# Gated linear attention on 64-row matmuls: halves of the array instead of zero-padded operands

## The reference, cut to what matters

```python
def gla_chunked(q, k, v, log_a):          # C = 64
    b = jnp.cumsum(gc, axis=-2)
    ref = b[..., C // 2 - 1:C // 2, :]
    q_in = qc * jnp.exp(b - ref)
    k_in = kc * jnp.exp(ref - b)
    A = jnp.where(mask, jnp.einsum('nbhid,nbhjd->nbhij', q_in, k_in), 0.0)
    o_intra = jnp.einsum('nbhij,nbhjv->nbhiv', A, vc)
    q_inter = qc * jnp.exp(b)
    k_state = kc * jnp.exp(b_last - b)
    decay = jnp.exp(b_last[..., 0, :])
    def step(state, inp):
        o = jnp.einsum('bhid,bhdv->bhiv', qi, state)
        state = state * di[..., None] + jnp.einsum('bhjd,bhjv->bhdv', ki, vi)

o_f = gla_chunked(q, k, v, la_f)
o_b = flip(gla_chunked(flip(q), flip(k), flip(v), flip(la_b)))
o = rmsnorm(o_f + o_b, out_norm)
```

## Time and profile before

| | |
|---|---|
| median of three runs | 2820.85 us (2816.14 to 2821.78) |
| profiled execution | span 2816.3 us from first to last instruction; 30040 instructions |
| PE busy | 2493.3 us, 89% of the span |
| PE weight loads | 1792.1 us, 64% |
| DVE busy | 1210.0 us, 43% |
| ACT busy | 984.3 us, 35% |
| POOL busy | 471.9 us, 17% |
| granted PE clock, mean | 0.948 |

### The profile page before, as it was taken

The page is one execution under the profiler, slowest core; times in us unless marked ns, Lnnn a source line. Parts: engine busy times, 40 slices in busy tenths (PEclk is TensorE's granted clock), DMA queues, the critical chain, the costliest instruction groups (busy, mean ns, idle before and its releaser), DMA issues. The chain is left out here.

```text
span 2816.3 us, 30040 instructions
## 1 busy us (share of the span) xinstructions
PE 2493.3 (89%) x10658; PEld 1792.1 (64%) x10658; DVE 1210.0 (43%) x1936; ACT 984.3 (35%) x1573; POOL 471.9 (17%) x506
## 2 busy tenths in 40 slices
PE   5997787938999958898999989998889899998997
PEld 4876465823444436787766667776777766666875
DVE  3379575241111144454235543523555215554433
ACT  3211575110111144554422232425555333223413
POOL 4157142021222123111100000002111110000000
PEclk9999899978999969999999999998999999999998
DMA  3201100146999851010110021101110120003101
GB/s 93 79 30 60 60 1 9 39 112 223 352 338 321 286 210 39 23 28 25 40 56 10 1 90 60 36 38 48 30 30 23 31 71 20 0 1 120 65 4 60
DMA packets 207016, 222.64 MB, mean 79 GB/s; under 512 B 50464, under 2 KB 170528, under 8 KB 206880
## 3 DMA queue, kind: packets, MB, share of 16 engines
q1 hardware_dynamic: 196400, 204.02, 22.3%
q0 software_dynamic: 9440, 16.83, 1.7%
q10 hardware_dynamic: 1040, 0.00, 0.0%
HBM read 203.41 MB, written 33.13 MB: 84 GB/s over the span
## 5 line engine op out<-in xcount | busy, mean ns | idle before, releaser
L106 PE MATMUL ps<-WT_lo,HT_hi 128*128 128x512 f32 x832 | 326.5, 392 | 0.0
L107 PE MATMUL ps<-HT_hi,WF_lo 128*128 128x512 f32 (+1 forms) x800 | 316.1, 395 | 0.0
L105 PE MATMUL ps<-HT_hi,WU_hi 128*128 128x512 f32 (+1 forms) x704 | 288.6, 410 | 15.8 <-DVE H_lo L2016 12.4
L106 PE MATMUL ps<-H_lo,WU_hi 128*128 128x512 f32 (+1 forms) x704 | 277.0, 394 | 0.0
L1463 PE MATMUL ps<-WT,MIX 128*128 128x512 f32 x496 | 226.1, 599 | 2.9 <-DVE MIX L1974 2.9
L105 PE MATMUL ps<-W_hi,HT_hi 128*128 128x512 f32 x512 | 212.3, 415 | 6.4 <-DVE MIX_lo L2153 6.4
L874 POOL TENSOR_TENSOR WF_lo<-WF,WU_hi 128x1024 fp32r<-128x1024 f32 (+1 forms) x44 | 116.2, 2640 | 607.8 <-ACT WU_hi L1079 607.8
L107 PE MATMUL ps<-W_hi,MIX_lo 128*128 128x512 f32 x512 | 200.9, 392 | 0.0
L427 POOL TENSOR_SCALAR ss<-ss 128x1 f32<-128x1 f32 x56 | 15.5, 277 | 1041.3 <-ACT ps L415 786.7
L106 PEld LDWEIGHTS ps<-WT_lo,HT_hi 128*128 128x128 f32 x832 | 158.2, 190 | 36.4 <-issue 5.3
L107 PEld LDWEIGHTS ps<-HT_hi,WF_lo 128*128 128x128 f32 (+1 forms) x800 | 151.9, 190 | 34.1
(11 more groups left out here) (395 smaller groups left out, 4854.4 us busy)
## 6 DMA issues: line engine op xcount, KB each, us to landing
WT<-in_w_gate SPq DMA_DIRECT2D x31, 1024.0 KB, 5.9
WT<-in_w_up SPq DMA_DIRECT2D x31, 1024.0 KB, 9.4
MIX<-in_w_down SPq DMA_DIRECT2D x31, 1024.0 KB, 8.7
WF<-in_w_in SPq DMA_DIRECT2D x48, 512.0 KB, 3.9
WT<-in_w_out SPq DMA_DIRECT2D x6, 2048.0 KB, 9.0
H<-in_x SPq DMA_DIRECT2D x16, 512.0 KB, 6.9
h_dram<-H SPq DMA_DIRECT2D x16, 512.0 KB, 3.4
H<-h_dram SPq DMA_DIRECT2D x16, 512.0 KB, 6.9
```

The costliest lines, as they stand in the source:

```text
L105: pe.matmul(o, lh, rh, start=(i == 0), stop=False)
L106: pe.matmul(o, lh, rl, start=False, stop=False)
L107: mm = pe.matmul(o, ll, rh, start=False, stop=(i == last))
```

## The change

`kf` and `kb` become one tile `k_in` written by one DVE instruction over all 128 partitions, `ks_even` and `ks_odd` one tile `ks` written by two ACT instructions in place of four. `inner` and `states` take 64 partitions of both operands per matmul: first partitions 0 to 63, then 64 to 127, in turns, into different PSUM banks. The number of matmuls in them stays 16 each. `causal` adds `Af` and `Ab` into `Asum` on DVE, and `outputs` does three matmuls for a tile in place of four. POOL's two memsets get half as wide.

```diff
-        kf, kb = slot(WTf, 0), slot(WTf, 1)
+        k_in = slot(WTf, 0)
-        ks_even, ks_odd, Af, Ab = (MIX[:, i, :] for i in range(4))
+        ks, Asum, Af, Ab = (MIX[:, i, :] for i in range(4))
+        kv_pairs = kv.rearrange("p (t r) v -> p t r v", r=2)
@@ POOL
-                pool.memset(WT[:, 0, :, :], 0.0).then_inc(z_ready, 1)
+                pool.memset(WT[:, 0, 4:KD, :], 0.0).then_inc(z_ready, 1)
-                pool.memset(MIX[:, 0:4, :], 0.0).then_inc(z_ready, 1)
+                pool.memset(MIX[:, 2:4, :], 0.0).then_inc(z_ready, 1)
@@ ACT
                 def ks_copy(h):
                     act.wait_ge(*gla(L, "kt", h))
-                    act.wait_ge(z_ready, L * 5 + 2)
+                    if h == 0:
+                        act.wait_ge(mx_lo, mx_at(L, 0, NT - 1))
                     for half in range(2):
-                        act.activation(ks_even[0:64, half * HALF:(half + 1) * HALF], ps[0:64, 6 + half, :], ACT.Copy)
-                        o = act.activation(ks_odd[64:P, half * HALF:(half + 1) * HALF], ps[64:P, 6 + half, :], ACT.Copy)
+                        o = act.activation(ks[:, half * HALF:(half + 1) * HALF], bank(6 + half), ACT.Copy)
                 def kv_copy(h):
                     for b in range(4):
-                        o = act.activation(kv[:, 4 * b:4 * b + 4, :], quads(2 + b), ACT.Copy)
+                        half, par = b % 2, b // 2
+                        o = act.activation(kv_pairs[:, 4 * half:4 * half + 4, par, :], quads(2 + b), ACT.Copy)
@@ PE
-                    for d, kk in enumerate((kf, kb)):
-                        for t in range(NT):
-                            mm = pe.matmul(bank(2 + 2 * d + t // 4, P, (t % 4) * P), kk[:, t * P:(t + 1) * P], q_in[:, t * P:(t + 1) * P], start=True, stop=True)
+                    for t in range(NT):
+                        ts = slice(t * P, (t + 1) * P)
+                        for d in range(2):
+                            r = slice(64 * d, 64 * d + 64)
+                            mm = pe.matmul(bank(2 + 2 * d + t // 4, P, (t % 4) * P), k_in[r, ts], q_in[r, ts], start=True, stop=True)
                     for c in range(NCH):
-                        t = c // 2
-                        mm = pe.matmul(bank(2 + c // 4, P, (c % 4) * P), (ks_even, ks_odd)[c % 2][:, t * P:(t + 1) * P], gv[h % 2][:, t * P:(t + 1) * P], start=True, stop=True)
+                        t, par = c // 2, c % 2
+                        r, ts = slice(64 * par, 64 * par + 64), slice(t * P, (t + 1) * P)
+                        mm = pe.matmul(bank(2 + 2 * par + t // 4, P, (t % 4) * P), ks[r, ts], gv[h % 2][r, ts], start=True, stop=True)
-                        mm = accumulate(pe, ..., [(gv[h % 2][:, ts], Af[:, ts]), (gv[h % 2][:, ts], Ab[:, ts]),
+                        mm = accumulate(pe, ..., [(gv[h % 2][:, ts], Asum[:, ts]),
@@ DVE
-                    dve.tensor_tensor(kf[0:64, :], gt[0:64, :], k[0:64, :], ALU.mult)
-                    dve.tensor_tensor(kb[64:P, :], gt[64:P, :], k[64:P, :], ALU.mult)
+                    dve.tensor_tensor(k_in, gt, k, ALU.mult)
@@ causal, behind the masked copies
+                    dve.wait_ge(*gla(L, "am", h))
+                    if h >= 1:
+                        dve.wait_ge(*gla(L, "o", h - 1))
+                    dve.tensor_tensor(Asum, Af, Ab, ALU.add)
```

More of the change, by code:

```diff
@@ L1567, in outputs @@
                         ts = slice(t * P, (t + 1) * P)
-                        mm = accumulate(pe, bank(6 + t // 4, P, (t % 4) * P), [(gv[h % 2][:, ts], Af[:, ts]), (gv[h % 2][:, ts], Ab[:, ts]),
+                        mm = accumulate(pe, bank(6 + t // 4, P, (t % 4) * P), [(gv[h % 2][:, ts], Asum[:, ts]),
                                                                              (st[:, 2 * t, :], q_even[:, ts]), (st[:, 2 * t + 1, :], q_odd[:, ts])])
```

## The result

The changed kernel takes 2775.85 us, median of four runs (2774.13 to 2778.56), against 2820.63 (2816.14 to 2821.78) for four runs of the kernel before. The medians are 44.8 us apart; 41.6 were forecast. The ratio of the runs is 0.9847 (95% interval 0.9835 to 0.9859), which is 43.2 us less (39.8 to 46.5). In the profiled executions the span went from 2816.3 to 2772.4 us.

A forecast was written before the change was run, and what follows sets the result against it. PE was taken to bound the stretch behind the heads, and within heads PE alternating with ACT/DVE chains. Terms: -18.5 without overlap, -25.7 and +2.6 with it, together -41.6 us from 2820.85, giving 2779 us; range 2769 to 2808.

The forecast's parts named there:

- Side by side: inner and states: matmuls on the two array halves run together, a tenth lost; -25.7 us over 16 stages.
- rivals 1 and 2: inner and states: single file, no gain there, 2805 us (chance 0.25); or half overlapped, 2791 us (chance 0.15).
- rival 3: inner and states: every change of row group empties the pipe; slower, 2844 us; chance 0.07.
- the low clock: inner(0): with PE's wait ahead shortened, the low clock may not come; 3.8 us saved in all.
- The pipe at a change of size: Changing between 128-row and 64-row matmuls may empty the pipe, at most 0.163 us each; +2.6 us taken.
- outputs: outputs: 16 of 64 records go; -3.6 us behind head 3, -1.4 us from head 2's slack.
- products: One DVE instruction less: -4.9 us ahead of inner(1) and inner(3), -6.5 ahead of inner(0), -3.8 from its clock.
- The memset: Second layer's start: POOL's L874 comes earlier, meets DVE's row split and delays the first unit; +1.7 us taken.
- the waits were to stay ahead of `inner(1)` and `inner(3)`: Sign: PE's waits ahead of these stages still ended by ACT L1181, a little longer than before.

The follow-up runs named there:

- g1: Kernel before with only inner and states put on 64 rows in turns; products, copies, memsets and outputs kept: 2792.02 us.
- e1: Changed kernel with four products a tile in outputs again, Af and Ab one by one, no Asum: 2782.78 us.
- e2: Changed kernel with k_in written by two DVE instructions of 64 partitions each: 2794.62 us.
- e4: Changed kernel with POOL's memset of WT back at its old width, 8 slots in place of 4: 2775.29 us.
- e3: Changed kernel with the same matmuls not in turns, all of rows 0 to 63 first, then 64 to 127: 2804.47 us.
- h1: Changed kernel with the first block's attention scores also on 64 rows, the two halves in turns: 2770.25 us.

## Why the prediction was right, term by term

**Side by side** (forecast -25.7, with +2.6 for an emptied pipe). Right in mechanism; rivals 1 and 2 fall with the record cuts, rival 3 with the stages of 2.06 us. A stage falls from 3.73 to 2.06, 1.67 and not the 1.79 of the full halving: the second pair starts 0.21 us behind the first, and only the later ones at steps of 0.112. The size was off the other way: g1, which has this step alone, gains 28.1 where the two terms made 23.1. Part of it is the low clock. `inner` lost 13.2 us to it before (43.0 in eight stages, where 8 x 3.73 would be 29.8) and loses 9.3 in g1 (25.8 for 16.5).

**The pipe at a change of size** (forecast +2.6). The price is there, and a little above the prediction's bound of 0.163 us a change. `states(3)` stands between two units and shows it at the full clock, before and after:

```profile
1329.39 0.39 PE L107 MATMUL ps<-HT_hi,WF_lo 128*128 128x512 f32 x1
1329.62 3.73 PE L1561 MATMUL ps<-WF,MIX 128*128 128x128 f32 x32
1333.10 0.48 PE L105 MATMUL ps<-HT_hi,WU_hi 128*128 128x512 f32 x1
```

```profile
1309.33 0.39 PE L107 MATMUL ps<-HT_hi,WF_lo 128*128 128x512 f32 x1
1309.65 2.06 PE L1566 MATMUL ps<-WF,MIX 64*128 64x128 f32 x32
1311.63 0.50 PE L105 MATMUL ps<-HT_hi,WU_hi 128*128 128x512 f32 x1
```

From the unit's record ahead to the one behind it takes 2.30 us in place of 3.71, so the stage saves 1.41, and 0.38 of the full 1.79 is missing: 0.19 for each of its two changes of size. The late second pair is part of it. If all 16 stages are like this one, they save 22.6 us (an estimate). The prediction took off a tenth and 2.6 us, to 23.1; the sum of its two terms was right, and what it called a tenth lost is this price. The Trainium skill, "TensorEngine Tiling (Array Packing)", section Key Properties, says that a change of tiling mode drains the engine. The trace agrees in that a change costs time, the 0.19 us; that it is a drain isn't shown.

**outputs** (forecast -3.6 and -1.4). By the start times, 1.43 and 2.22 us behind the two heads 3, together 3.6. At head 2 the slack of 0.51 us a layer is used up, 1.0 in all, and PE now waits 0.34 and 0.33 there. Right but for 0.4; e1 agrees. `Asum` is hidden as said, in the wait of the earlier trace rows:

```profile
1300.17 1.23 DVE L2075 TENSOR_TENSOR MIX<-MIX 128x1024 f32<-128x1024 f32 x1
...
1313.85 0.34 DVE L2085 SCALAR_TENSOR_TENSOR WT<-WT,marks 64x128 f32<-64x128 f32 x1 [12.46 <-ACT WT L1167]
```

**products** (forecast -4.9, -6.5, -3.8). products(1) and (3) got shorter by 5.3. products(0) gave 3.39 and 3.37, 6.8 in all, and DVE did get in ahead of POOL. The clock at `inner(0)` stayed up in both layers, and e2's `inner(0)` is slowed by 1.72 (3.78 against 2.06), as the 3.8 for two layers has it. e2 takes all three away at once and costs 18.8, where the terms have 15.2. But its stretches split it otherwise: 6.6 us are waiting, where the first two terms have 11.4 (DVE's time came as forecast, but less of it was PE's), and 10.4 are the low clock, where the third has 3.8. The low clock reached more than `inner(0)`; its `inner(1)` is slowed by 1.62.

**The memset** (forecast +1.7). PE's wait ahead of the unit grew from 5.67 to 7.61, 1.9 us. Right at its place; in e4's median it can't be seen.

**What was missed.** First the low clock: 3.8 us were forecast, at `inner(0)` alone, and in the stretches about 8.5 came. In part the loss went, in part it moved: `inner` loses 0.4 us to it (16.9 for 16.5) in place of 13.2, and `squares` is busy 6.5 more. Second, the waits were to stay ahead of `inner(1)` and `inner(3)`, a little longer than before. This sign didn't come: ahead of `inner` PE waits 18.4 us less, ahead of `squares` 11.6 more, for the wait was cut in two. Third, a faster `inner` ran into a wait nobody had seen, the transposes' for DVE's `finish`: 4.0 us by the page.

The parts measured alone are 28.1 + 18.8 + 6.9 = 53.8 us, the whole is 44.8, and the whole alone pays the memset's 1.9; so 7.1 us are counted twice. By the stretches it is 27.2 + 17.0 + 7.1 = 51.3 against 48.1, 3.2 us. Neither is far above the noise. Where they overlap is the low clock: by PE's busy time in the stretches it gives 8.8 us in g1 (31.4 less the 22.6 of work), 10.4 in e2 and 1.0 in e1, 20.2 together, but 8.5 in the whole. These are estimates from one profile each, and waits make up for a part of it. That the forecast was only 3 us off rests in part on errors that cancelled: the low clock's gain too small, what DVE's time is worth to PE too large, the transposes left out. ACT's two copies less and the narrower memset of MIX had no run of their own.

## What to carry to other kernels

Zero padding that picks a part of the contraction rows can be exchanged for 64-row matmuls, here in 2.06 us in place of 3.73, but only if neighbours in the program lie on different halves; the same matmuls in another order gain nothing (e3). A stage that PE is the bound of pays in full; where another engine hands over at each step (h1), most of it turned into waiting. And before costing a saving on PE, ask what its next wait is and whether it runs at the low clock: a wait split in two and a wait in one piece can leave different stages slow, so parts measured alone need not add up.

## What the runs showed that I had not expected

- Two weight loads of 188 ns on the two halves run beside each other, so that a pair costs 0.112 us with its loads.
- Each change between 128-row and 64-row matmuls cost about 0.19 us at `states(3)`.
- In the twelve profiles, each of the 27 waits of PE of 4.42 to 6.12 us ahead of a stage of the heads was followed by a low clock in that stage. After shorter waits it went either way, so their length alone doesn't settle it. `gates(1)` to `gates(3)`, always behind 2.15 to 2.60 us of waiting, took anything from 1.98 to 3.78. In the first layer of the changed kernel a wait of 3.12 was followed by `inner(1)` at 2.06, with 2.13 us of waiting and a slowed `squares` ahead of it; in e3 much the same pair, 2.15 and 3.17 us, was followed by a slow `inner(1)`:

```profile
1171.41 2.72 PE L1580 MATMUL ps<-X,ones 128*128 128x512 f32 x4 [2.15 <-ACT X L1175]
...
1183.65 6.51 PE L1551 MATMUL ps<-X,WT 64*128 64x128 f32 x32 [3.17 <-ACT X L1183]
```

- Where a 128x1024 subtraction of POOL (2.4 us alone) met a DVE product in these rows, the two took turns, and the one that came second took longer: on DVE's side 3.27 us in place of 1.23 (`la`) and 3.44 in place of 1.29 (the pair of L2059), on POOL's 2.96 to 3.04.
